# Stored activations moved in 2 KB rows two blocks at a time, and the gate loads of the weighted sum put on ScalarE's DMA queue

## The chip, the core and the metric

One core of one Trainium2 chip. The time is device microseconds of one execution, lower is better. TensorE (PE), VectorE (DVE), ScalarE (ACT), GpSimd (POOL) and SyncE (SP) run their own instruction streams and meet at semaphores; SP, ACT and POOL issue DMAs, each into a queue of its own (q1, q10 and q0 in the profile), and the core's 16 DMA engines serve all three queues.

## The reference, cut to what matters

The program is one inference step of a two-layer network on 384 tokens (128 context, 256 latent) of width 1024. Each layer ends in an expert stage:

```python
q = (x @ w_q).reshape(T, PEER_HEADS, 2, PEER_HALF)          # 8 heads, two halves
s1, i1 = lax.top_k(s[:, :, 0], PEER_TOPK)                   # 16 of 128 keys, each half
...
idx = ...                                                   # 128 of 16384 experts per token
g = jax.nn.softmax(top_s, axis=-1)
uc = jnp.take(u_tab, ic, axis=0)
a = jnp.einsum('cd,ckd->ck', xc, uc)
wgt = gc * jax.nn.gelu(a, approximate=False)
vc = jnp.take(v_tab, ic, axis=0)
return jnp.einsum('ck,ckd->cd', wgt, vc)
```

Both expert tables, u and v, have 16384 rows of 1024 floats (64 MB each, per layer).

## The kernel before

The kernel computes the expert stage in two ways at once.

For the 128 context tokens (the sparse side) POOL gathers, for each of 128 slots, the u row and the v row of every token in one indirect DMA: 128 rows of 8 KB, 1 MB, into one of four buffers that the profile names hf, work, uv_stat and hots (`gather`). DVE takes the dot product with the token (`step`, line 1383), ACT bends it (`weight`, lines 923 and 925), and DVE adds the weighted v row (`add_row`, line 1375), which frees the buffer for a gather four slots later.

For the 256 latent tokens (the dense side) all 16384 experts are evaluated, 128 blocks of 128 experts. A layer's expert stage has these parts:

- **u blocks.** SP loads a block of u (128 rows of 4 KB, 512 KB) into one of four `raw` slots; ACT and POOL split it into a high and a low half (`high`, line 677, and `low`, line 585); PE multiplies; ACT applies GELU (`gelu`, line 908) and stores the block's 128x256 activations in a DRAM tensor `a_dram` (line 910). The slot of `ga` that the GELU writes is one of four, so a GELU waits for the store of four blocks earlier.
- **the table part**, blocks 32 to 95: beside each block PE builds one-hot products of the gates of four tokens, ACT copies them to a staging tile and every eight blocks stores a chunk of the gates to `g_dram` (lines 954 and 955). A gather goes with every second block.
- **the tail**, blocks 96 to 127: no table work, a gather with every block.
- **the sweep**: for each of 128 blocks of v, DVE multiplies the block's activations by its gates (`tt` in `sweep`, line 1423, 128x256, called w below), and PE adds w times v into PSUM (line 1729, four matmuls of 128x512 floats, eight records in the profile). SP loads the v blocks (line 452) four ahead. The activations come back from `a_dram` into four slots of `a_in`: ACT reloads a slot as soon as the w that reads it is done (line 970, 128 rows of 1 KB). The gates come back from `g_dram` for four blocks at a time into two halves of `g_in` (line 542, 1024 pieces of 512 B, 512 KB). SP issues that load after the v load which follows a half's fourth block on PE. A w waits for its slot of `a_in`, for its half of `g_in`, and for the PE block four earlier. A gather goes with every second block.

In the sweep of layer 0 fourteen of the sixteen rounds of eight blocks also load four blocks of `mod_w` of 512 KB (SP, line 554), which DVE reduces (line 1034, twice per block). So a round moves 8 v blocks, 4 gathers, 8 activation blocks, 2 gate halves and 4 mod blocks in layer 0, and the same without the mod blocks in layer 1.

Every queue works in the order in which its engine issues. ACT's program in the sweep is `beside`: in each group of two blocks it waits for w, issues a reload, runs `weight` for the gather of that group, and so on.

Of the kernel before, what the change touches and what calls it, by code (L numbers as in the profile page):

```python
# [33 lines left out]
F32 = mybir.dt.float32  # L34
# [142 lines left out]
def build(nc, io):  # L177
    ctx = ExitStack()
    with ctx:
# [3 lines left out]
        def sem(name):  # L183
            return ctx.enter_context(nc.semaphore(name))
# [64 lines left out]
        mod_w = hots[:, :].rearrange("p (s d) -> p s d", s=MSLOTS)  # L249
        c_all = keys[:, :, :].rearrange("p a k -> p (a k)").rearrange("p (g d) -> p g d", g=2)  # L250
        unread = ga[:, :, :].rearrange("p a t -> p (a t)")[:, 0:D].bitcast(BF16).rearrange("p (g d) -> p g d", g=2)

# [122 lines left out]
        s_taken = sem("s_taken")  # L375
        a_stored = [sem(f"a_stored{j}") for j in range(4)]
        top_ready = sem("top_ready")
# [7 lines left out]
        g_stored = [sem(f"g_stored{j}") for j in range(2)]  # L385
        a_loaded = [sem(f"a_loaded{j}") for j in range(4)]
        g_loaded = [sem(f"g_loaded{j}") for j in range(2)]
# [26 lines left out]

        a_dram = nc.dram_tensor("a_dram", (N_KEYS, P, ND), F32).ap()
        g_dram = nc.dram_tensor("g_dram", (NCHUNK, P, N_KEYS * CHUNK), F32).ap()
# [23 lines left out]
        def _(sp):  # L440
# [63 lines left out]
            for layer in range(DEPTH):  # L504
# [10 lines left out]
                sp.wait_ge(cols_done, layer + 1)  # L515
                for j in range(4):
                    sp.wait_ge(a_stored[j], 16 * (layer * (N_KEYS // 4) + 1))
                    sp.dma_start(a_in[:, j, :], one(a_dram, j)).then_inc(a_loaded[j], 16)
                for s in range(2):
# [3 lines left out]
                for s in range(2):  # L523
                    sp.wait_ge(g_stored[s], 16 * (layer + 1) * (NCHUNK // 2))
                for j in range(4):
                    sp.wait_ge(a_stored[j], 16 * (layer + 1) * (N_KEYS // 4))
# [6 lines left out]
                def beside(i, j, more):  # L533

                    sp.wait_ge(block_done, i * 8 + (v0 + j + 1))
                    if more or j < 8 - RING:
                        load(name, i * 8 + (j + RING), v0 + j)
                    elif after:
                        load(after, j - (8 - RING), v0 + j)
                    if more and j % 4 == 3:  # L540
                        s = j // 4
                        sp.dma_start(g_in[:, s].unsqueeze(1),
                                     g_quads[:, bass.ds(i * 2 + (s + 2), 1)]).then_inc(g_loaded[s], 16)

# [117 lines left out]
        def _(act):  # L662
# [208 lines left out]
            def scores(layer):  # L871
                m0, r0 = M0[f"wq{layer}"], R0[f"wq{layer}"]
                for j in range(4 if layer else 0):
                    act.wait_ge(a_stored[j], 16 * (N_KEYS // 4))
# [28 lines left out]
            def gelu(layer, i, step, m, r, count):  # L903

                j = count % 4
                projected(i, step, m)
                since(act, a_stored[j], i * (4 * step) + 16 * (layer * N_KEYS // 4 + count // 4))
                nc.scalar.activation(ga[:, j, 0:ND], ps[:, PROJ + r % 2, 0:ND], ACT.Gelu).then_inc(proj_taken, 1)  # L908
                act.wait_ge(proj_taken, i * step + (r + 1))
                act.dma_start(one(a_dram, i * step + count), ga[:, j, 0:ND]).then_inc(a_stored[j], 16)  # L910

            def experts(layer):
# [53 lines left out]
                def beside(i, last):  # L966
                    for j in range(8):
                        if j < 4 or not last:
                            act.wait_ge(w_ready, i * 8 + (layer * N_KEYS + j + 1))
                            act.dma_start(a_in[:, j % 4, :], one(a_dram, i * 8 + (j + 4))).then_inc(a_loaded[j % 4], 16)  # L970
                        if j % 2 == 0:
                            weight(i, 4, TABLE_STEPS + TAIL + j // 2)
# [30 lines left out]
        def _(dve):  # L1003
# [409 lines left out]
            def sweep(layer):  # L1413
# [3 lines left out]
                def eight(i, mods):  # L1417
                    for j in range(8):
                        dve.wait_ge(a_loaded[j % 4], i * 32 + (16 * (base // 4 + j // 4 + 1)))
                        if j % 4 == 0:  # L1420
                            dve.wait_ge(g_loaded[j // 4], i * 16 + 16 * (base // 8 + 1))
                        dve.wait_ge(block_done, i * 8 + (v0 + j - WBUFS + 1))
                        tt(wf[:, j % WBUFS, :].rearrange("p (c t) -> p c t", t=CHUNK),  # L1423
                           a_in[:, j % 4, :].rearrange("p (c t) -> p c t", t=CHUNK),
                           g_in[:, j // 4, :, (j % 4) * CHUNK:(j % 4 + 1) * CHUNK], ALU.mult).then_inc(w_ready, 1)
                        if j % 2 == 0:
                            step(layer, i, 4, TABLE_STEPS + TAIL + j // 2)
                        if mods:
                            mod_group(i, MSLOTS, MOD_EARLY - MSLOTS, j // 2, j % 2, mod_late)
# [3 lines left out]
                if layer == 0:  # L1433
                    eight(0, False)
                    settle(nc.vector.memset(a_pad, 0.0))
                    dve.wait_ge(c_ready, 3)
                    for j in range(4):
                        dve.wait_ge(a_stored[j], 16 * (N_KEYS // 4))
# [405 lines left out]
```

## Time and profile before

| | before |
|---|---|
| median of 3 runs | 2580.07 us (2576.76 to 2583.82) |
| the profiled execution | 2576.08 us, span 2573.8 us |
| table part and tail, layer 0 | about 411 to 775 us of the span |
| sweep, layer 0 | about 793 to 1252 us |
| table part and tail, layer 1 | about 1723 to 2090 us |
| sweep, layer 1 | 2109 to 2554 us |
| granted TensorE clock, mean | 0.96 |

The profiled execution is one run of the program, so its own time stands beside its span; 2.3 us lie outside the span. A share of the DMA engines can pass 1, because the records of packets that follow each other on an engine overlap a little.

### The profile page before, as it was taken

To read this page: it belongs to the slowest core of one execution; us is meant where nothing else is said; L and a number is where in the kernel's file an instruction comes from. 1 tells how busy PE (TensorE), PEld (TensorE's weight loads), DVE (VectorE), ACT (ScalarE), POOL (GpSimd) and SP (SyncE) were. 2 spreads that over 40 slices of the span, in tenths; PEclk is the share of its full clock that TensorE was granted. 3 is DMA by queue.
4 is the path that set the end of the run, shared out by engine and by line. 5 is a ranking of instruction groups with operands and counts; after the bars stand their busy time and mean duration, and the time that the engine had idled before them with its cause. 6 is when DMAs were issued, how large, how long until landed. Compare 5 with 4: busy or idle time off the path is not lost.

```text
span 2573.8 us, 40077 instructions
## 1 busy us (share of the span) xinstructions
PE 2300.8 (89%) x11829; PEld 1701.6 (66%) x11829; DVE 1772.7 (69%) x3945; ACT 916.1 (36%) x1702; POOL 1131.7 (44%) x612
## 2 busy tenths in 40 slices
PE   6687999999777989899977889999999769999998
PEld 3676999999773333333467479989998754444443
DVE  7986798888555666666679856888886554444444
ACT  3254445666441111111042453656665420000001
POOL 2623587777782222222145035677777851111110
PEclk8898999999998999999998989999999989999999
DMA  7423378999999999999922023579999999999995
GB/s 295 158 91 116 121 226 306 388 385 382 404 420 396 394 394 394 394 394 394 351 99 90 1 66 115 180 254 368 384 383 384 420 374 370 371 380 381 379 378 206
DMA packets 284090, 771.10 MB, mean 300 GB/s; under 512 B 26080, under 2 KB 160352, under 8 KB 248544
## 3 DMA queue, kind: packets, MB, share of 16 engines
q1 hardware_dynamic: 169664, 401.76, 43.6%
q0 software_dynamic: 36864, 268.45, 25.7%
q10 hardware_dynamic: 77472, 99.78, 10.7%
q8 instruction: 45, 0.74, 0.1%
q14 instruction: 45, 0.37, 0.0%
HBM read 701.08 MB, written 68.81 MB: 299 GB/s over the span
## 4 chain that ended last, share of the span: by engine, by line
PE 54%; DMA 16%; issue 15%; DVE 8%; POOL 4%; SPq 2%; ACT 1%; ACTq 0%; DVEq 0%; POOLq 0%
PE ps L1729 25%; DMA raw<-in_v 7%; PE ps L1495 7%; PE ps L1496 7%; PE ps L1497 7%; PE ps L1711 4%; POOL w_lo L585 4%; DMA work<-in_uv,picked 2%; DMA hf<-in_uv,picked 2%; SPq L554 1%; DMA uv_stat<-in_uv,picked 1%; DMA hots<-in_uv,picked 1%; DVE ga L1034 1%; DVE ps L1375 1%; DMA work<-g_dram 1%
## 5 line engine op out<-in xcount | busy, mean ns | idle before, releaser
L585 POOL TENSOR_TENSOR w_lo<-raw,w_hi 128x1024 fp32r<-128x1024 f32 x330 | 823.1, 2498 | 575.6 <-ACT w_hi L677 573.3
L1729 PE MATMUL ps<-raw,work 128*128 128x512 f32 x2048 | 902.8, 602 | 69.4 <-DMA raw<-in_v 42.5
L1495 PE MATMUL ps<-h_hi,w_hi 128*128 128x256 f32 (+1 forms) x2560 | 781.0, 305 | 92.8 <-POOL w_lo L585 79.6
L1729 PEld LDWEIGHTS ps<-raw,work 128*128 128x128 f32 x2048 | 390.8, 192 | 580.1 <-issue 574.8
L1496 PE MATMUL ps<-h_lo,w_hi 128*128 128x256 f32 (+1 forms) x2560 | 758.3, 296 | 0.0
L1497 PE MATMUL ps<-h_hi,w_lo 128*128 128x256 f32 (+1 forms) x2560 | 758.1, 296 | 0.0
L1495 PEld LDWEIGHTS ps<-h_hi,w_hi 128*128 128x128 f32 x2560 | 495.6, 194 | 112.1 <-POOL w_lo L585 97.4
L1496 PEld LDWEIGHTS ps<-h_lo,w_hi 128*128 128x128 f32 x2560 | 496.2, 194 | 0.0
L1497 PEld LDWEIGHTS ps<-h_hi,w_lo 128*128 128x128 f32 x2560 | 494.9, 193 | 0.0
L677 ACT ACTIVATE w_hi<-raw 128x1024 fp32r<-128x1024 f32 x330 | 348.5, 1056 | 117.5 <-DMA raw<-in_in 36.4
L1423 DVE TENSOR_TENSOR work<-work 128x256 f32<-128x256 f32 x256 | 106.2, 421 | 409.4 <-DMA work<-g_dram 320.9
L923 ACT ACTIVATE wgt<-dots (+1 forms) x256 | 53.2, 208 | 683.9 <-DVE hf L1383 226.6
L603 POOL DMA_INDIRECT hots<-in_uv,picked x64 | 74.5, 1164 | 408.9 <-DVE ps L1375 390.7
L1402 DVE TENSOR_SCALAR hots<-ps,work 128x128 f32<-128x128 f32 x512 | 173.7, 400 | 0.0
L944 ACT ACTIVATE work<-ps 128x512 f32<-128x512 f32 x128 | 145.3, 1135 | 79.5 <-PE ps L1711 64.7
L908 ACT ACTIVATE ga<-ps 128x256 f32<-128x256 f32 x256 | 97.6, 381 | 193.7 <-PE ps L1497 183.5
L603 POOL DMA_INDIRECT work<-in_uv,picked x64 | 71.0, 1110 | 176.5 <-DVE ps L1375 165.8
L1398 DVE TENSOR_TENSOR hots<-ps,work 128x512 f32<-128x512 f32 x128 | 87.9, 687 | 80.4 <-PE ps L1711 80.3
L1034 DVE CUSTOM_DVE_ANT_0 ga<-work,keys 128x1024 bf16<-128x1024 f32 x112 | 136.2, 1216 | 0.0
L1711 PE MATMUL ps<-hots 128*128 128x128 f32 x1024 | 135.4, 275 | 0.0
L603 POOL DMA_INDIRECT uv_stat<-in_uv,picked x64 | 70.9, 1108 | 139.7 <-DVE ps L1375 137.0
L1711 PEld LDWEIGHTS ps<-hots 128*128 128x128 f32 x1024 | 125.6, 192 | 0.4 <-issue 0.2
(195 smaller groups left out, 2315.3 us busy)
## 6 DMA issues: line engine op xcount, KB each, us to landing
raw<-in_u SPq DMA_DIRECT2D x256, 512.0 KB, 6.8
raw<-in_v SPq DMA_DIRECT2D x256, 512.0 KB, 8.9
a_dram<-ga ACTq DMA_DIRECT2D x256, 128.0 KB
work<-g_dram SPq DMA_DIRECT2D x64, 512.0 KB, 11.3
work<-a_dram ACTq DMA_DIRECT2D x248, 128.0 KB, 8.9
g_dram<-work ACTq DMA_DIRECT2D x16, 1920.0 KB, 10.6
work<-in_mod_w SPq DMA_DIRECT2D x56, 512.0 KB, 11.0
hots<-in_mod_w SPq DMA_DIRECT2D x32, 512.0 KB, 3.6
```

The source lines that it names most:

```text
L585: nc.gpsimd.tensor_tensor(w_lo[:, m % RING, :], raw[:, m % RING, :], w_hi[:, m % RING, :].bitcast(F32), ALU.subtract).then_inc(lo_ready, 1)
L603: nc.gpsimd.indirect_dma_start(out=uv_rows[q % UVBUFS], out_offset=None, in_=io[f"uv{layer}"], in_offset=bass.IndirectOffsetOnAxis(ap=pick ...
L677: nc.scalar.activation(w_hi[:, m % RING, :], raw[:, m % RING, :], ACT.Copy).then_inc(hi_ready, 1)
L944: nc.scalar.activation(stage[:, s, :, tok:tok + TOK].rearrange("p k t -> p t k"), ps[:, ACC, :].rearrange("p (t k) -> p t k", k=N_KEYS), A ...
L1034: nc.vector.tensor_tensor_reduce(unread[:, g, :], ring[:, k, :], c_all[:, g, :], 1.0, 0.0, ALU.mult, ALU.add, accum_out=sums[:, k, g:g + 1 ...
L1402: last = ts(oh1[:, b, q, :], iota_p, col_key[:, 0, tok], col_g[:, tok], ALU.is_equal, ALU.mult)
L1423: tt(wf[:, j % WBUFS, :].rearrange("p (c t) -> p c t", t=CHUNK), a_in[:, j % 4, :].rearrange("p (c t) -> p c t", t=CHUNK), g_in[:, j // 4, ...
L1495: mm(out, w_hi[:, s, cols], h_hi[:, k, first:], start=n == 0, stop=False)
L1496: mm(out, w_hi[:, s, cols], h_lo[:, k, first:], start=False, stop=False)
L1497: last = mm(out, w_lo[:, s, cols], h_hi[:, k, first:], start=False, stop=n == KC - 1)
L1711: last = mm(ps[:, ACC, q * P:(q + 1) * P], oh2[:, b, q, :], oh1[:, b, q, :], start=True, stop=True)
L1729: last = mm(ps[:, Y_DENSE[NT - ND_TILES + t] + half, :], wf[:, b, t * P:(t + 1) * P], raw[:, s, half * 512:(half + 1) * 512], start=first, ...
```

## The change

Two things are changed. First, activations travel in pairs. `a_dram` has one row of 2 KB for two blocks where it had two of 1 KB. The GELU of an even block stores nothing; that of the odd block stores both. Reloads too are for two blocks, issued after the w of the odd one. There are two store semaphores and two load semaphores where there were four each. Second, the gate loads of the sweep (but for the first two of a layer) move from SP's program into ACT's `beside`: they are issued behind the reload that follows w of a half's fourth block, where SP issued them after PE had finished that block.

```diff
+        a_out = ga[:, :, :].rearrange("p a t -> p (a t)")[:, 0:4 * ND].rearrange("p (a t) -> p a t", a=4)
...
-        a_dram = nc.dram_tensor("a_dram", (N_KEYS, P, ND), F32).ap()
+        a_dram = nc.dram_tensor("a_dram", (N_KEYS // 2, P, 2 * ND), F32).ap()
...
-                for j in range(4):
+                for j in range(2):
                     sp.wait_ge(a_stored[j], 16 * (layer * (N_KEYS // 4) + 1))
-                    sp.dma_start(a_in[:, j, :], one(a_dram, j)).then_inc(a_loaded[j], 16)
+                    sp.dma_start(a_in[:, 2 * j:2 * j + 2, :].rearrange("p a t -> p (a t)"),
+                                 one(a_dram, j)).then_inc(a_loaded[j], 16)
...
-                    if more and j % 4 == 3:
-                        s = j // 4
-                        sp.dma_start(g_in[:, s].unsqueeze(1),
-                                     g_quads[:, bass.ds(i * 2 + (s + 2), 1)]).then_inc(g_loaded[s], 16)
...
-                since(act, a_stored[j], i * (4 * step) + 16 * (layer * N_KEYS // 4 + count // 4))
-                nc.scalar.activation(ga[:, j, 0:ND], ps[:, PROJ + r % 2, 0:ND], ACT.Gelu).then_inc(proj_taken, 1)
-                act.wait_ge(proj_taken, i * step + (r + 1))
-                act.dma_start(one(a_dram, i * step + count), ga[:, j, 0:ND]).then_inc(a_stored[j], 16)
+                pair = count // 2 % 2
+                since(act, a_stored[pair], i * (4 * step) + 16 * (layer * N_KEYS // 4 + count // 4))
+                nc.scalar.activation(a_out[:, j, :], ps[:, PROJ + r % 2, 0:ND], ACT.Gelu).then_inc(proj_taken, 1)
+                if count % 2:
+                    act.wait_ge(proj_taken, i * step + (r + 1))
+                    act.dma_start(one(a_dram, i * (step // 2) + count // 2),
+                                  a_out[:, j - 1:j + 1, :].rearrange("p a t -> p (a t)")).then_inc(a_stored[pair], 16)
...
-                        if j < 4 or not last:
+                        if j % 2 and (j < 4 or not last):
                             act.wait_ge(w_ready, i * 8 + (layer * N_KEYS + j + 1))
-                            act.dma_start(a_in[:, j % 4, :], one(a_dram, i * 8 + (j + 4))).then_inc(a_loaded[j % 4], 16)
+                            act.dma_start(a_in[:, j % 4 - 1:j % 4 + 1, :].rearrange("p a t -> p (a t)"),
+                                          one(a_dram, i * 4 + (j // 2 + 2))).then_inc(a_loaded[j // 2 % 2], 16)
+                        if j % 4 == 3 and not last:
+                            s = j // 4
+                            act.dma_start(g_in[:, s].unsqueeze(1),
+                                          g_quads[:, bass.ds(i * 2 + (s + 2), 1)]).then_inc(g_loaded[s], 16)
...
-                        dve.wait_ge(a_loaded[j % 4], i * 32 + (16 * (base // 4 + j // 4 + 1)))
+                        if j % 2 == 0:
+                            dve.wait_ge(a_loaded[j // 2 % 2], i * 32 + (16 * (base // 4 + j // 4 + 1)))
```

ACT's program in the sweep, before, from a round's start (line 970 is the activation reload, 923 and 925 are `weight`):

```order
L970 ISA [waits w_ready]
L970 DMA work<-a_dram 128x256
L922 ISA
L923 ISA [waits dot_done]
L923 ACT_TABLE_LOAD
L923 ACTIVATE wgt<-dots 128x1
L925 REGISTER_ALU [waits bent]
L925 ACTIVATE wgt<-wgt,gate_s 128x1
L969 REGISTER_ALU
L970 ISA [waits w_ready]
L970 DMA work<-a_dram 128x256
```

The same program with the change, from the wait for a half's fourth w (line 971 is the reload of a pair, 975 the gate load):

```order
L971 ISA [waits w_ready]
L971 DMA work<-a_dram 128x512
L975 ISA
L975 DMA work<-g_dram 128x8x128
L923 REGISTER_ALU
L924 ISA [waits dot_done]
L924 ACTIVATE wgt<-dots 128x1
L926 REGISTER_ALU [waits bent]
L926 ACTIVATE wgt<-wgt,gate_s 128x1
L970 REGISTER_ALU
L971 ISA [waits w_ready]
L971 DMA work<-a_dram 128x512
```

ACT waits for w once in two blocks and no longer ahead of a round's first `weight`; the gate load stands right behind a reload, and the next pair's reload is behind it in the queue.

SP's program in the sweep of layer 0, before, from the v load that follows a half's third block (line 452 is a v load, 542 the gate load, 554 a mod load):

```order
L452 ISA [waits block_done]
L452 DMA raw<-in_v 128x1024
L535 REGISTER_ALU
L452 ISA [waits block_done]
L452 DMA raw<-in_v 128x1024
L542 ISA
L542 DMA work<-g_dram 128x8x128
L553 REGISTER_ALU
L554 ISA [waits mod_summed]
L554 DMA work<-in_mod_w 128x1024
```

With the change SP's loop has v loads (line 453) and mod loads (line 552) alone:

```order
L453 ISA [waits block_done]
L453 DMA raw<-in_v 128x1024
L537 REGISTER_ALU
L453 ISA [waits block_done]
L453 DMA raw<-in_v 128x1024
L551 REGISTER_ALU
L552 ISA [waits mod_summed]
L552 DMA work<-in_mod_w 128x1024
```

Nothing of SP's queue but the gate load has moved.

ACT's program in the tail, before (line 908 is the GELU, 910 the store, 677 the high half of a later block):

```order
L908 ACTIVATE ga<-ps 128x256 [waits a_stored1,block_done]
L910 DMA a_dram<-ga 128x256 [waits proj_taken]
L923 ACTIVATE wgt<-dots 128x1 [waits dot_done]
L925 ACTIVATE wgt<-wgt,gate_s 128x1 [waits bent]
L677 ACTIVATE w_hi<-raw 128x1024 [waits block_done,raw_ready2]
L908 ACTIVATE ga<-ps 128x256 [waits a_stored2,block_done]
L910 DMA a_dram<-ga 128x256 [waits proj_taken]
```

And with the change (907 is the GELU, 675 the high half):

```order
L907 ACTIVATE ga<-ps 128x256 [waits a_stored0,block_done]
L924 ACTIVATE wgt<-dots 128x1 [waits dot_done]
L926 ACTIVATE wgt<-wgt,gate_s 128x1 [waits bent]
L675 ACTIVATE w_hi<-raw 128x1024 [waits block_done,raw_ready1]
L907 ACTIVATE ga<-ps 128x256 [waits a_stored0,block_done]
L910 DMA a_dram<-ga 128x512 [waits proj_taken]
```

The GELU of an even block now waits for a store that was issued three blocks earlier, where every GELU waited for one issued four blocks earlier.

## Rows read from the trace of the kernel before

**Rows 1.** Windows: busy us per engine, granted clock, DMA share, GB/s

```profile
420.00:640.00 220.00, 220.00 (x1870) 219.92 (x1869) 180.29 (x381) 150.35 (x234) 167.57 (x89) 1.00 0.98 376
660.00:780.00 120.00, 91.14 (x693) 85.67 (x694) 68.69 (x85) 51.06 (x113) 94.52 (x57) 0.99 1.02 419
838.00:1220.00 382.00, 343.26 (x767) 146.24 (x765) 257.82 (x445) 39.27 (x108) 80.13 (x48) 0.98 1.04 394
...
2230.00:2550.00 320.00, 319.10 (x741) 139.60 (x740) 143.50 (x230) 22.88 (x92) 42.49 (x43) 1.00 0.99 368
```

**Rows 2.** The chain that ended last, 930 to 1000 us

```profile
932.46 4.68 SPq L554
937.39 11.49 DMA raw<-in_v
...
949.01 14.01 PE ps L1729 x32
...
963.72 0.38 SPq L542
964.36 5.09 SPq L554
969.71 11.14 DMA raw<-in_v
```

**Rows 3.** PE in time order, 949 to 982 us: start, length, idle before

```profile
949.01 13.99 PE L1729 MATMUL ps<-raw,work 128*128 128x512 f32 x32 [1.77 <-DMA raw<-in_v]
965.17 14.00 PE L1729 MATMUL ps<-raw,work 128*128 128x512 f32 x32 [2.16 <-DMA raw<-in_v]
```

**Rows 4.** DMA queues, 950 to 982 us: packets, MB, share of 16 engines

```profile
q1 hardware_dynamic: 3815, 7.37, 62.2%
q0 software_dynamic: 576, 4.19, 32.4%
q10 hardware_dynamic: 1152, 1.05, 9.5%
```

**Rows 5.** DMA queues, 700 to 750 us, in the tail of layer 0

```profile
q0 software_dynamic: 1753, 12.76, 60.6%
q1 hardware_dynamic: 1796, 6.55, 32.2%
q10 hardware_dynamic: 1739, 1.59, 9.1%
```

**Rows 6.** The chain that ended last, 2075 to 2112 us

```profile
2092.67 0.40 SPq L518
2093.12 0.45 SPq L518
2093.61 0.44 SPq L518
2094.10 0.44 SPq L518
2094.54 0.05 issue
2094.64 13.35 DMA work<-g_dram
```

**Rows 7.** Waits, 665 to 785 us, and the same for 1985 to 2100 us

```profile
ACT ga L908 <- DMA a_dram<-ga: 4.1, 3, 1.7
...
ACT ga L908 <- DMA a_dram<-ga: 5.5, 4, 1.7
```

**Rows 8.** Waits, 838 to 1220 us: total us, times, longest

```profile
DVE work L1423 <- DMA work<-g_dram: 94.3, 13, 7.7
...
PE ps L1729 <- DMA raw<-in_v: 36.8, 19, 2.4
```

**Rows 9.** DMA queues, 974 to 976 us, while gate pieces cross a gather

```profile
q0 software_dynamic: 75, 0.61, 75.1%
q1 hardware_dynamic: 77, 0.11, 15.0%
q10 hardware_dynamic: 77, 0.08, 11.1%
```

**Rows 10.** Gate loads (line 542), 2200 to 2500 us

```profile
DMA to landing us min/median/max: 5.2/8.4/12.1
```

**Rows 11.** DVE in time order, 2303 to 2306 us: a w and one gather's two steps

```profile
2303.27 0.42 DVE L1423 TENSOR_TENSOR work<-work 128x256 f32<-128x256 f32 x1 [11.09 <-DMA work<-g_dram]
2303.61 1.21 DVE L1383 SCALAR_TENSOR_TENSOR hf<-hf,ps 128x1024 f32<-128x1024 f32 x1
2304.75 0.08 DVE L1383 DVE_READ_ACCUMULATOR hf<-hf,ps  x1
2304.75 1.28 DVE L1375 SCALAR_TENSOR_TENSOR ps<-hots,wgt,ps 128x1024 f32<-128x1024 f32 x1
```

More of the change, by code:

```diff
@@ L375, in build @@
         s_taken = sem("s_taken")
-        a_stored = [sem(f"a_stored{j}") for j in range(4)]
+        a_stored = [sem(f"a_stored{j}") for j in range(2)]
         top_ready = sem("top_ready")
@@ L385, in build @@
         g_stored = [sem(f"g_stored{j}") for j in range(2)]
-        a_loaded = [sem(f"a_loaded{j}") for j in range(4)]
+        a_loaded = [sem(f"a_loaded{j}") for j in range(2)]
         g_loaded = [sem(f"g_loaded{j}") for j in range(2)]
@@ L524, in _ @@
                     sp.wait_ge(g_stored[s], 16 * (layer + 1) * (NCHUNK // 2))
-                for j in range(4):
+                for j in range(2):
                     sp.wait_ge(a_stored[j], 16 * (layer + 1) * (N_KEYS // 4))
@@ L872, in scores @@
                 m0, r0 = M0[f"wq{layer}"], R0[f"wq{layer}"]
-                for j in range(4 if layer else 0):
+                for j in range(2 if layer else 0):
                     act.wait_ge(a_stored[j], 16 * (N_KEYS // 4))
@@ L1436, in sweep @@
                     dve.wait_ge(c_ready, 3)
-                    for j in range(4):
+                    for j in range(2):
                         dve.wait_ge(a_stored[j], 16 * (N_KEYS // 4))
```

## The prediction

> **What bounds the kernel now.** I first read the windows by stage [rows 1], because the two edits touch only the expert stages. The reader is to see three kinds of stage there. In the table part (420 to 640 us) PE is busy for the whole window; the DMA engines are nearly full too, but PE sets the pace. In the tail (660 to 780) PE is busy 91 of 120 us and the DMA share is 1.02 at 419 GB/s. In the sweep of layer 0 PE is busy 343 of 382 us with a share of 1.04 at 394 GB/s; in that of layer 1 PE is busy 319.1 of 320 us, and the share is 0.99.
>
> So the sweep of layer 1 holds 0.9 us of idle PE in 320: nothing can be won there but at its start. The one stage with idle PE and moved instructions is the sweep of layer 0. The chain of the end [rows 2] goes there through a v load that SP issued late: SP issued the gate load at 963.72, then stood 5.09 us in the issue of a mod load, and only at 969.71 could the v load begin for which PE waited until 980.85. PE in time order [rows 3] shows 14.0 us of work for four blocks, then about 2 us idle: 16 per half round (965.17 - 949.01 is 16.2), 32 per round. Read alone, this says that the gate load in SP's queue costs 4 us a round.
>
> The DMA queues of the same round [rows 4] say otherwise. The shares sum to 62.2 + 32.4 + 9.5 = 104.1%: all 16 engines work through the whole round, the 2 us in which PE waits included. That is what I take as the limit: 12.6 MB in 32 us. An order of issues that lets the v loads come earlier makes a gather or a gate load come later, and all of them must come within the round, because DVE and the four buffers of each kind let nothing run more than some four blocks ahead.
>
> **The change part by part.** The sum is made against the profiled execution's 2576.08 us (span 2573.8); the median shown is 2580.07, 4 us above it, and I carry the difference over to the median.
>
> *Rows of 2 KB.* No load in the trace has rows of 2 KB, so I interpolate. From the steady tail [rows 5], in which each queue has nearly one size of row: q10 (1 KB) used 9.1% of 16 x 50 = 800 us, 72.8 us for 1590 KB, 45.8 ns per KB; q1 (4 KB) 257.6 us for 6550 KB, 39.3 ns; q0 (8 KB) 484.8 us for 12760 KB, 38.0 ns. A cost of 8.9 ns per row and 37.1 ns per KB fits the first two and gives 38.2 for the third. For 2 KB rows it gives 41.4, that is 4.4 ns less per KB. The ends: no saving at all, or a row as cheap as the 8 KB ones (7.8 ns per KB). In a round of layer 0's sweep the activations are 1049 KB, so 4.6 us of engine time, over 16 engines 0.29 us; fourteen such rounds give **4.0 us**. In the tail, also DMA-bound, a block stores 131 KB: 0.036 us, for 32 blocks in two layers **2.3 us**. In the table part and layer 1's sweep the saving lies beside a busy PE: nothing; it only widens the DMA's slack, by which the next paragraphs are covered.
>
> The Trainium skill (DMA: Bandwidth & Descriptors, Specifications) puts the smallest transfer that runs at line rate at 512 B. By it rows of 1 KB are already at full rate, and the first two terms are nothing; the rows above show 1 KB rows 17% dearer per KB than 4 KB rows, so I don't follow it, but it is a rival below in its own right.
>
> *Fewer issues.* At the start of a sweep SP issues four activation loads, 0.44 us each, ahead of the gate load for which the chain waits in layer 1 [rows 6]. Two of them go: **0.9 us** in layer 1. In layer 0 I count nothing (bound: another 0.9). The issues that ACT loses (four a round) and gains (two a round) are of this kind, some 0.4 us each [rows 2, 6], on an engine that is idle most of the sweep (39 of 382 us busy [rows 1]).
>
> *Stores in pairs.* A GELU's buffer is now asked for three blocks after its store instead of four. In the tail four blocks are just enough at the start, behind the last store of gates: ACT waited for a store 3 times, 4.1 us together, in layer 0 and 4 times, 5.5 us, in layer 1 [rows 7], and nowhere later. A block of the tail takes 4.1 us (12.76 MB of gathers, 1.05 MB each, in 50 us [rows 5]), so at those places the wait can grow by up to 4.1 us. The DMA engines have gathers and u blocks to work on meanwhile, so most of it is covered; I charge **1 us** in all. In the table part PE has a second product buffer, so a GELU can be late by nearly a block's work before PE waits.
>
> *Gate loads on ACT's queue.* The bytes are the same, so in layer 0 the price is nothing as long as the engines stay full. What the move does is to the waits. DVE waits for gates 94.3 us in twelve rounds [rows 8], because SP asks for them only when PE is through the half; ACT can ask when the w is made, up to three blocks sooner. That wait should go or turn into a shorter one for either tensor. But SP's stall behind the gate load goes, ACT gets the stall in its place (behind it: `weight`, for which DVE's next gathered row waits), and the loads compete differently. While gate pieces cross a gather [rows 9] each queue gets the same number of packets, 75 to 77 in 2 us, whatever their size: a 512 B piece costs a turn, in which an 8 KB row passes too. On q10 a gate load (64 pieces per engine) now has two other queues to share with. I take 0, covered by the lead of w.
>
> The sum: 4.0 + 2.3 + 0.9 - 1 = 6.2 us less: 2569.9 for an execution like the profiled one, **2574** for the median. With the ends of the row price (nothing; 7.1 + 4.1 us) the forecast's own range is 2568 to 2580.
>
> **The rivals.**
>
> *SP unblocked pays in full (faster).* If the DMA share of 1.04 hides slack and PE's waits come from the order alone, the waits for v [rows 8], 36.8 us in twelve rounds, go: 43 us for fourteen, 2537; half of it gives 2558. For it: the chain passes through SP's stall. Against it: rows 4 show no free engine time, and the tail's 419 GB/s is reached with longer rows. The Trainium skill says in the same page (Issuing engines are not separate DMA queues) that spreading DMAs over issuing engines saves only issue time. By that this rival is at most the stall itself, where it is not bandwidth.
>
> *The gates starve on q10 (slower).* In layer 1 a half's load is issued after its fourth w and wanted by the w five blocks on; a round is 8 blocks, 28 us at PE's pace (3.5 us each [rows 3]). Between the landing and the next issue for that half lie four w and two gather steps, 4 x 0.42 + 2 x 2.57 = 6.8 us of DVE [rows 11]. So it decides at a landing time of 21 us; each us above costs a us per round, 15 per layer. Before, it was 8.4 us in the median and 12.1 at most [rows 10]. 64 turns at 2 us / (76 / 16) = 0.42 us are 27 us, if both other queues never run dry. Against that: in layer 1 they do, the share being 0.99 of a possible 1.04. At 23 us it would cost 30 us, 2604. By the Trainium skill (same page, Queues, rings and completion order) an engine drains a packet of 9 to 17 descriptors before it turns to another queue; then this rival would be impossible. Rows 9 show single records in turn, so I keep it.
>
> *The store distance (slower).* If a store in the tail's steady part takes over three blocks (12.3 us) but under four, which rows 7 allow, every second GELU is late, and with it the high halves, POOL's low halves and the gathers behind them in POOL's program. At 1 us per pair it is 16 pairs x 2 = 32 us, less the gain: 2606. Against it: q10 passes as many packets as the others in the tail [rows 5], and half of them go, so its backlog should drain.
>
> *The size of a row gives nothing (no change).* Then 2579.
>
> **How the numbers follow.** A measurement of this kernel can tell some 0.3%, 7.7 us, from no change. The forecast gets 0.58; its centre is 1.6 us short of that bound, so I split it 0.20 faster, 0.37 same, 0.01 slower. SP unblocked gets 0.16 (0.15 faster), starved gates 0.10 (0.09 slower), the store distance 0.07 (0.04 slower), no gain from rows 0.09 (0.08 same). Faster 0.36, same 0.50, slower 0.14. The range 2558 to 2590 holds the forecast, half of the first rival and the small ends of the slower ones; it leaves out about 0.18.
>
> **What would show it.** Right: in layer 0's sweep the round shrinks from 32.0 us by some 0.3, the shares still sum to 1.04, and PE still idles near 4 us a round, though SP no longer stands behind a gate load. DVE's wait for gates falls from 94 us in that window by over half. In the tail q10 has half the packets, at about 41 ns per KB. PE stays over 99% busy in layer 1's sweep. Wrong: a round of 29 to 30 us (SP unblocked); PE under 98% in layer 1's sweep with DVE waiting for gates over 20 us after their issue (starved); waits of ACT for stores all through the tail with a block over 4.1 us (store distance).

## The result and the profile after

The changed kernel takes 2622.37 us in the median of 4 runs (2611.35 to 2622.97), the kernel before 2581.95 in the median of its 4. The ratio is 1.0149, with a 95% interval of 1.0123 to 1.0176: slower by 40 us between the medians, where 2574 was forecast with a range of 2558 to 2590. The time is outside the range and on the other side of the kernel before.

The windows by stage of the kernel after, the same stretches as [rows 1]:

```profile
420.00:640.00 220.00, 220.00 (x1871) 220.00 (x1870) 180.62 (x383) 151.35 (x236) 167.29 (x89) 1.00 0.98 377
660.00:780.00 120.00, 92.00 (x692) 86.33 (x690) 69.30 (x87) 51.30 (x112) 93.87 (x57) 0.97 1.02 420
838.00:1220.00 382.00, 321.62 (x695) 138.05 (x694) 229.99 (x397) 35.51 (x97) 71.74 (x43) 0.93 0.95 355
2230.00:2550.00 320.00, 320.00 (x747) 142.10 (x746) 148.14 (x234) 23.38 (x94) 44.93 (x47) 1.00 1.02 382
```

In three of the four rows PE is as busy as before. The third, the sweep of layer 0, is not: the DMA share fell from 1.04 to 0.95 and PE finished 695 matmul records in 382 us instead of 767. A round of eight blocks is 64 records, so the rate gives 35.2 us per round after (382 x 64 / 695) and 31.9 before. From the first matmul of that sweep to the last, PE's rows show 543.5 us where they showed 499.9 (+43.6), some 3.1 us in each of the fourteen rounds. The stretch between the sweeps took 810.3 instead of 815.1 us (-4.8), the sweep of layer 1 442.1 instead of 444.7 (-2.6); with 0.7 us less ahead of the first sweep this is the 35.4 us between the two profiled spans, 2609.2 and 2573.8. (The table of before gives the sweep of layer 0 up to about 1252 us; its last matmul in fact ended at about 1294.)

The mean granted clock in that window fell too, from 0.98 to 0.93 of 2.4 GHz. In the kernels below it is 0.97 to 1.00 where the share is 1.04, 0.95 to 0.97 where it is 1.02 or 1.03, and 0.91 in the slowest. The chain that ended last between 1040 and 1115 us holds no piece of PE at all, so I count no loss of its own for the clock; no run separates the two.

The page's chain names the new cause. Before, DMA of `work<-a_dram` was not in its list; after it is second:

```profile
PE ps L1736 17%; DMA work<-a_dram 12%; PE ps L1502 7%; PE ps L1503 7%; PE ps L1504 6%; PE ps L1718 4%; POOL w_lo L583 3%; DVE ga L1040 3%; DMA work<-in_uv,picked 2%; DVE ps L1381 2%; DMA hots<-in_uv,picked 1%; DMA hf<-in_uv,picked 1%; DMA uv_stat<-in_uv,picked 1%; DVE ps L1328 1%; DVE work L1330 1%
```

The waits of the kernel after, 838 to 1220 us (total us, times, longest), beside [rows 8]:

```profile
DVE work L1430 <- DMA work<-a_dram: 147.4, 19, 12.8
...
PE ps L1736 <- DVE work L1430: 54.6, 10, 8.9
...
PE ps L1736 <- DMA raw<-in_v: 5.7, 7, 1.4
```

DVE (w is line 1430 now) no longer waits for gates; it waits for *activations*, 147 us, where it waited 94 for gates. PE's waits for v fell from 36.8 to 5.7 us, but ten waits for w of up to 8.9 us took their place. The DMA issues of the same window (KB each, median us from issue to landing) say what is late:

```profile
work<-g_dram ACTq DMA_DIRECT2D x22, 512.0 KB, 19.3
...
work<-a_dram ACTq DMA_DIRECT2D x43, 256.0 KB, 10.9
```

And the chain that ended last, 1040 to 1115 us, shows where that sits in a round:

```profile
1050.41 21.13 DMA work<-a_dram
...
1075.93 1.22 DVE ga L1040
...
1078.63 1.20 DVE ps L1381
1079.84 1.13 DVE ga L1040
...
1083.93 1.20 DVE ps L1381
1085.13 1.13 DVE ga L1040
1086.27 0.35 DVE work L1430
1086.77 19.21 DMA work<-a_dram
```

A reload of a pair takes 21.13 us to land. Then DVE works 15 us through w's, gather steps (line 1381) and mod reductions (line 1040) until it has made the w behind which ACT may issue the reload of the same place in the next round, which takes 19.21 us again. 1086.77 - 1050.41 = 36.4 us: a closed loop of one reload and 15 us of DVE per round, longer than the 32 us that the bytes need (the next one takes 35.1 us). In DVE's time order the 15 us hold six w's, three gathers' two steps and five mod reductions, without a gap. ACT's program says why that reload is late, in time order:

```profile
1045.67 0.42 ACTq L975 DMA_DIRECT2D work<-g_dram  x1
...
1050.41 0.35 ACTq L971 DMA_DIRECT2D work<-a_dram  x1
```

It was issued 4.7 us behind a gate load, in the same queue. DVE in time order stood 12.16 us for it:

```profile
1071.77 0.42 DVE L1430 TENSOR_TENSOR work<-work 128x256 f32<-128x256 f32 x1 [12.16 <-DMA work<-a_dram]
```

and PE 5.73 us behind DVE:

```profile
1072.25 4.64 PE L1736 MATMUL ps<-raw,work 128*128 128x512 f32 x5 [5.73 <-DVE work L1430]
```

### The profile page after: what moved, and what is told of

It reads as the page before. It is cut to its first block, busy times and chain, and to the rows that moved or that the text cites. A ratio compares the mean times of both kernels' runs of the same rounds, so it can differ in the third digit from the quotient of the medians.

```text
span 2609.2 us, 39322 instructions
## 1 busy us (share of the span) xinstructions
PE 2309.4 (89%) x11829; PEld 1712.3 (66%) x11829; DVE 1783.1 (68%) x3945; ACT 912.6 (35%) x1702; POOL 1125.7 (43%) x612
## 4 chain that ended last, share of the span: by engine, by line
PE 43%; DMA 20%; DVE 16%; issue 15%; POOL 3%; ACT 1%; DVEq 1%; ACTq 0%; SPq 0%; POOLq 0%
PE ps L1736 17%; DMA work<-a_dram 12%; PE ps L1502 7%; PE ps L1503 7%; PE ps L1504 6%; PE ps L1718 4%; POOL w_lo L583 3%; DVE ga L1040 3%; DMA work<-in_uv,picked 2%; DVE ps L1381 2%; DMA hots<-in_uv,picked 1%; DMA hf<-in_uv,picked 1%; DMA uv_stat<-in_uv,picked 1%; DVE ps L1328 1%; DVE work L1330 1%
## 5 line engine op out<-in xcount | busy, mean ns | idle before, releaser
L1736 PE MATMUL ps<-raw,work 128*128 128x512 f32 x2048 | 912.5, 608 | 100.0 <-DVE work L1430 94.0
L1736 PEld LDWEIGHTS ps<-raw,work 128*128 128x128 f32 x2048 | 398.4, 196 | 612.8 <-issue 523.1
L601 POOL DMA_INDIRECT hf<-in_uv,picked x64 | 70.9, 1107 | 150.1 <-DVE ps L1381 147.0
## 6 DMA issues: line engine op xcount, KB each, us to landing
g_dram<-work ACTq DMA_DIRECT2D x16, 1920.0 KB, 11.1
```

The lines of the kernel that those rows point to most:

```text
L601: nc.gpsimd.indirect_dma_start(out=uv_rows[q % UVBUFS], out_offset=None, in_=io[f"uv{layer}"], in_offset=bass.IndirectOffsetOnAxis(ap=pick ...
L1736: last = mm(ps[:, Y_DENSE[NT - ND_TILES + t] + half, :], wf[:, b, t * P:(t + 1) * P], raw[:, s, half * 512:(half + 1) * 512], start=first, ...
```

## The experiments

The theory after the result: a gate load is 1024 pieces of 512 B, 64 on each DMA engine, and each costs its queue a turn. On ACT's queue the pair's reload stands behind these turns, and in layer 0 DVE's share of the loop is long, because the mod reductions are in it. The rivals: that the pairs do it (rows of 2 KB, the store distance, two slots asked for at a time); that the reload behind the gates is at fault and the order in the queue would mend it; that the load on DVE or on the DMA engines alone has grown. Of each kernel below the text names the window 838 to 1220 us of layer 0's sweep, unless it says otherwise. Ratios are against the kernel before on the same chip, whose median was 2581.2, 2581.9 and 2581.9 us in the three groups of runs.

**pairs_only**: the change without the move of the gate loads.

```diff
+                    if more and j % 4 == 3:
+                        s = j // 4
+                        sp.dma_start(g_in[:, s].unsqueeze(1),
+                                     g_quads[:, bass.ds(i * 2 + (s + 2), 1)]).then_inc(g_loaded[s], 16)
...
-                        if j % 4 == 3 and not last:
-                            s = j // 4
-                            act.dma_start(g_in[:, s].unsqueeze(1),
-                                          g_quads[:, bass.ds(i * 2 + (s + 2), 1)]).then_inc(g_loaded[s], 16)
```

> The pairs of blocks and the 2 KB rows, with the gate loads back in SP's program. Theory A (the reload of a pair waits in ScalarE's queue behind the gate load, and DVE's next round waits for it): layer 0's round is DMA-bound again, 31.5 to 32 us instead of 35; the time is 2 to 10 us under the kernel before, ratio 0.996 to 1.000. Theory B (the pairs are at fault: a reload is asked for one w later and lands as a whole): most of the 40 us stay, ratio 1.010 or more. Theory C (both edits share the loss): ratio near 1.007.

2570.46 us (2567.32 to 2574.19), ratio 0.9958 (0.9944 to 0.9971). The pairs cost nothing and save some 11 us. Its windows:

```profile
838.00:1220.00 382.00, 347.58 (x773) 148.09 (x772) 258.05 (x445) 39.26 (x108) 79.76 (x48) 0.97 1.04 398
```

and its waits:

```profile
DVE work L1430 <- DMA work<-g_dram: 86.6, 14, 8.3
```

The share is back at 1.04, and DVE waits for gates as in [rows 8], with a gate load landing in 11.3 us on SP's queue.

**gates_only**: the kernel before with nothing but the move of the gate loads; rows of 1 KB, one block at a time.

```diff
-                    if more and j % 4 == 3:
-                        s = j // 4
-                        sp.dma_start(g_in[:, s].unsqueeze(1),
-                                     g_quads[:, bass.ds(i * 2 + (s + 2), 1)]).then_inc(g_loaded[s], 16)
...
+                        if j % 4 == 3 and not last:
+                            s = j // 4
+                            act.dma_start(g_in[:, s].unsqueeze(1),
+                                          g_quads[:, bass.ds(i * 2 + (s + 2), 1)]).then_inc(g_loaded[s], 16)
```

> Single blocks and 1 KB rows as before, with the gate loads on ScalarE's queue behind the reload of a half's fourth block. Theory A: the reload of the next block stands behind the gate load, so the loss is there, ratio 1.010 to 1.018, DVE waiting some 10 us a round in layer 0 for activations or gates. Theory B: the loss is gone, ratio 0.998 to 1.002. Theory C: near 1.007.

2622.09 us (2615.56 to 2623.76), ratio 1.0153 (1.0136 to 1.017): all of the loss, without a single 2 KB row. Its windows:

```profile
838.00:1220.00 382.00, 323.11 (x685) 137.27 (x684) 229.34 (x397) 35.50 (x97) 71.78 (x43) 0.92 0.96 357
```

and its waits:

```profile
DVE work L1423 <- DMA work<-a_dram: 150.6, 11, 15.1
```

The two halves of the change are not additive. Alone the move costs 1.53% and the pairs give 0.42%, together it is 1.49%. On top of the pairs the move thus costs some 1.9%, about 50 us. A likely reason, only argued: where the loop through DVE sets the round, bytes that cross faster are worth little.

**gate_rows_4k**: the kernel after, but ACT's gate load brings its 512 KB as 128 rows of 4 KB from one place of `g_dram` (the gates are then not those of the block, so the weighted sum differs).

```diff
-                            act.dma_start(g_in[:, s].unsqueeze(1),
-                                          g_quads[:, bass.ds(i * 2 + (s + 2), 1)]).then_inc(g_loaded[s], 16)
+                            act.dma_start(g_in[:, s].rearrange("p c t -> p (c t)"),
+                                          one(g_dram, 0)[:, 0:NCHUNK * QUAD * CHUNK]).then_inc(g_loaded[s], 16)
```

> The changed kernel, but every gate load issued by ScalarE reads 128 rows of 4 KB (the same 512 KB, from one place of the stored gates) instead of 1024 pieces of 512 B; the gates that it multiplies are thus not the right ones. Theory A, in which a piece costs a turn between the queues: 8 turns instead of 64, the gate load lands in under 12 us instead of 19, layer 0's round falls to the DMA bound, which is itself 1 us lower for 1792 fewer records a round: ratio 0.987 to 0.995. If the turn plays no part and the load is slow for its bytes or its place: landing near 19 us, ratio near 1.015.

2558.91 us (2558.01 to 2560.56), ratio 0.9914 (0.9899 to 0.9929). Same bytes, same queue, same place in it, an eighth of the pieces. Its DMA issues:

```profile
work<-g_dram ACTq DMA_DIRECT2D x25, 512.0 KB, 11.1
```

and its waits:

```profile
DVE work L1430 <- DMA work<-a_dram: 13.3, 7, 2.7
```

The landing falls from 19.3 to 11.1 us, DVE's wait from 147 to 13 us. So it is the cut into small pieces, not the queue or the order as such. The edit also reads one place of DRAM over and over; that alone did not make records short, as a 4 KB record of this load held its engine 168 ns and one of SP's loads from fresh places 165.

By the Trainium skill (DMA: Bandwidth & Descriptors, Specifications) pieces of 512 B are already at line rate. The trace's packet records decide against it: in this window of the kernel after, a 512 B piece held its engine 28.6 ns, so eight of them 229 ns against the 168 of one 4 KB record. For two gate loads a round that is 58.6 against 43.0 us of engine time, 1.0 us over 16 engines. It accounts for a quarter of the 3.8 us by which the round is shorter here (31.4 by the 779 records); the rest is the shorter landing.

**mod_sums_short**: the kernel after, with DVE reducing 64 of the 1024 columns of each later mod block (the sums of `mod` are then partial); the loads stay whole.

```diff
-                nc.vector.tensor_tensor_reduce(unread[:, g, :], ring[:, k, :], c_all[:, g, :], 1.0, 0.0,
+                n = 64 if ring is mod_late else D
+                nc.vector.tensor_tensor_reduce(unread[:, g, 0:n], ring[:, k, 0:n], c_all[:, g, 0:n], 1.0, 0.0,
```

> The changed kernel, but DVE reduces only 64 of 1024 columns of each mod block in layer 0's sweep (all loads are kept; the later modulation values are thus wrong). Theory A, a loop of queue time and DVE's ordered work (w, gather steps, mod reductions of 1.2 us each): with some seven reductions less in the loop the round falls from 35 us to the DMA bound near 32, ratio 0.998 to 1.003. If the loss is in the queues alone, whatever DVE does: the round stays near 35, ratio 1.012 or more.

2578.17 us (2575.18 to 2583.43), ratio 0.9993 (0.9984 to 1.0002). The loads are as slow as after, and the loop is shorter. Its windows:

```profile
838.00:1220.00 382.00, 339.55 (x751) 145.74 (x751) 164.83 (x446) 39.27 (x108) 48.32 (x48) 0.96 1.02 388
```

and its chain, 1040 to 1115 us:

```profile
1044.58 21.05 DMA work<-a_dram
...
1077.06 22.05 DMA work<-a_dram
```

21 to 22 us of landing are still on the chain, but the same reload comes every 32.5 us instead of every 36.4. So DVE's reductions are part of the loop. DVE waits for activations even longer than after, 207.4 us in this window, and the kernel is as fast as before: the sum of its waits is no measure of the loss. The edit has one side effect that it does not separate: POOL's gather instructions take 1.01 us on average instead of 1.67. 751 records give a round of 32.6 us, not the 31.6 of pairs_only: the queue's part is still just long enough to be felt.

**mod_loads_small**: the kernel after, with SP loading 64 of 1024 columns of each later mod block (so `mod` is made from stale columns); DVE reduces all columns. The load is still of 128 pieces, each of 256 B instead of 4 KB.

```diff
-                                sp.dma_start(mod_late[:, j // 2, :], one(io["mod_w"], i * MSLOTS + (MOD_EARLY + j // 2))
+                                sp.dma_start(mod_late[:, j // 2, 0:64],
+                                             one(io["mod_w"], i * MSLOTS + (MOD_EARLY + j // 2))[:, 0:64]
```

> The changed kernel, but in layer 0's sweep SP loads 64 of 1024 columns of each further mod block; DVE still reduces all 1024 columns (of old data, so the later modulation values are wrong). Theory A, a loop of queue time plus some 15 us of DVE's ordered work: DVE's part stays, the queue part falls towards the 13 us that a gate load takes in layer 1, so the round is near 28 us and bound by PE; ratio 0.970 to 0.980 (14 rounds less 7 us of after is 98 us from 2622). If DVE's work alone were the bound the round would stay at 35.

2514.38 us (2511.16 to 2518.29), ratio 0.9738 (0.9724 to 0.9752). Its windows:

```profile
838.00:1220.00 382.00, 382.00 (x891) 169.14 (x890) 300.74 (x514) 45.04 (x127) 90.99 (x55) 1.00 1.04 388
```

and its DMA issues:

```profile
work<-g_dram ACTq DMA_DIRECT2D x27, 512.0 KB, 11.4
```

PE is busy for the whole window. The queue order, the full DVE loop and the number of pieces are as after, but the four mod loads of a round bring 0.13 MB instead of 2.1, and a gate load lands in 11.4 us. So neither a long DVE loop nor the gates on ACT's queue lose time alone; the two need long records on the other queues. The edit also lowers the time that a round's bytes need, and does not separate this from the sooner turns.

**gates_behind**: the kernel after, with each gate load issued behind a reload that the next w's need, not ahead of it: after the sixth and eighth w of a round.

```diff
-                        if j % 4 == 3 and not last:
-                            s = j // 4
+                        if j in (5, 7) and not last:
+                            s = (j - 5) // 2
```

> The changed kernel, but the gate load of the first half is issued behind the reload of the pair that the same w will need (after the sixth w instead of the fourth). Theory A1 (w needs both, and whatever stands last in ScalarE's queue ends its wait): the reload lands in under 12 us, but the gates, asked for 5 us later, land as late as the reload did: DVE's wait is now for the gates, round 35 us or more, ratio 1.012 to 1.022. Theory A2 (only the reload's place behind the gate load hurts): round near 32, ratio 1.000 to 1.005.

2643.61 us (2634.4 to 2645.45), ratio 1.0231 (1.0213 to 1.0249), slower yet. Its waits change their name and hardly their length:

```profile
DVE work L1430 <- DMA work<-g_dram: 134.0, 10, 16.2
...
DVE work L1430 <- DMA work<-a_dram: 18.6, 9, 3.4
```

Now the gate load itself, 19.6 us from issue to landing, ends the wait. This reordering within ACT's queue does not mend the loss. It also asks for the gates two blocks later than the kernel after, three w's ahead of their use instead of five, so the run does not say what the order alone is worth.

**gates_sp_early**: pairs_only, with SP issuing the gate load two blocks earlier, behind a wait for w instead of for PE.

```diff
-                    if more and j % 4 == 3:
+                    if more and j % 4 == 1:
                         s = j // 4
+                        sp.wait_ge(w_ready, i * 8 + (layer * N_KEYS + j + 3))
```

> Pairs as in pairs_only, gate loads in SP's queue, but asked for as early as the changed kernel does: after the w of a half's fourth block instead of after its PE block. Theory A (the queue that they share, not the time at which they are asked for): as pairs_only, ratio 0.994 to 0.999, DVE's wait for gates in layer 0 falls from 87 us to under 40. If asking early crowds out the v loads: PE waits for v, layer 0's round 33 us or more, ratio 1.003 or more.

2580.33 us (2573.36 to 2586.08), ratio 0.9995 (0.9984 to 1.0006). DVE's wait for gates falls from 86.6 to 21.0 us and the rounds get no shorter. DVE waits for PE instead, 92.7 us where pairs_only has 6.4, and PE's wait for v goes from 26.6 to 34.2 us:

```profile
DVE work L1431 <- PE ps L1737: 92.7, 34, 7.2
...
PE ps L1737 <- DMA raw<-in_v: 34.2, 19, 3.4
DVE work L1431 <- DMA work<-g_dram: 21.0, 11, 2.6
```

So the 94 us that DVE waited for gates before [rows 8] were not a cost. Why it is some 10 us behind pairs_only is not settled. Its steady round is as long between w's of the rounds 3 to 15 (31.8 us in both), though its window has 759 records instead of 773 and a granted clock of 0.95 instead of 0.97; and from the 113th w to the last it takes 57.8 us, where pairs_only takes 48.4.

**before_again** and **pairs_only_again**: the two kernels unchanged, to see what such differences are worth.

> The kernel before once more, under a label of its own: ratio 1.000 within 0.002. Its profile shows how far the stages of one and the same kernel differ between two executions; pairs_only's profiled execution was 5 us faster than that of before, its median 10.7 us. If the profiled execution shown for before was a fast one of its kind, this one has 3 to 6 us more, spread over stages that no edit touches.

> pairs_only once more, beside the other two on the same chip: ratio 0.994 to 0.9975, and 102 us for the first 32 blocks of layer 1.

2579.93 us, ratio 0.9997 (0.9988 to 1.0007); and 2572.26, ratio 0.9962 (0.9947 to 0.9976), in another group of runs than pairs_only with 0.9958. The gain of the pairs repeats. Of the two profiles of the kernel before, one has a round of 31.9 us by its records (767 in 382 us), the other 31.8 (770); pairs_only and its repetition have 31.6 (773 both).

**reload_pairs**: pairs_only, with the stores single again (1 KB into one half of a 2 KB row, four semaphores); only the reloads are of 2 KB.

```diff
-                if count % 2:
-                    act.wait_ge(proj_taken, i * step + (r + 1))
-                    act.dma_start(one(a_dram, i * (step // 2) + count // 2),
-                                  a_out[:, j - 1:j + 1, :].rearrange("p a t -> p (a t)")).then_inc(a_stored[pair], 16)
+                act.wait_ge(proj_taken, i * step + (r + 1))
+                half = slice(count % 2 * ND, (count % 2 + 1) * ND)
+                act.dma_start(one(a_dram, i * (step // 2) + count // 2)[:, half], a_out[:, j, :]).then_inc(a_stored[j], 16)
```

> Gate loads in SP's queue; only the reloads are of pairs (2 KB rows); every block is stored by itself again, as 1 KB halves of the 2 KB rows, with four store semaphores. It splits pairs_only's gain. Theory D (the reloads give 0.2 us a round in layer 0's sweep, and the stores give 3 us at the start of layer 1's expert stage, where ACT's own issues lie in the chain): the first 32 blocks of layer 1 take 105 us as before, not 102; the round is 31.75 us; ratio 0.997 to 0.9995, less gain than pairs_only by 3 to 6 us. If the stores play no part: ratio 0.995 to 0.9965, as pairs_only.

2573.47 us (2570.03 to 2577.5), ratio 0.997 (0.9959 to 0.9981), against 0.9962 for pairs_only_again beside it. The two intervals overlap: between the medians the paired stores give 1.2 us, and anything from nothing to some 7 us would fit. The profiles show a difference in the first 32 u blocks of layer 1, in which ACT is on the chain before. Windows over exactly these blocks, of the kernel before:

```profile
1621.00:1726.00 105.00, 96.92 (x767) 93.88 (x766) 92.09 (x348) 64.01 (x80) 80.51 (x36) 0.98 0.72 232
```

and of pairs_only:

```profile
1618.50:1720.50 102.00, 94.85 (x766) 93.43 (x765) 97.07 (x346) 62.25 (x80) 80.24 (x36) 0.98 0.74 240
```

The same 80 instructions of ACT and the same matmuls take 3 us less. In the chain of before, 1640 to 1700 us, ACT's store issue (line 910) holds 6.9%; with half the issues DVE's top-k leads there. From the 1st GELU of layer 1 to the 33rd it is 104.9 us in both profiles of the kernel before and in reload_pairs, 102.0 in both of pairs_only, and 102.0 to 103.0 in the other kernels with paired stores. So the profiles give these 2 to 3 us to the paired stores; the medians neither confirm nor exclude it.

**gates_by_layer**: pairs_only, with SP issuing the gate loads in layer 0 and ACT in layer 1.

```diff
-                    if more and j % 4 == 3:
+                    if more and j % 4 == 3 and not layer:
...
+                        if j % 4 == 3 and not last and layer:
+                            s = j // 4
+                            act.dma_start(g_in[:, s].unsqueeze(1),
+                                          g_quads[:, bass.ds(i * 2 + (s + 2), 1)]).then_inc(g_loaded[s], 16)
```

> Pairs, with the gate loads in SP's queue in layer 0 and in ScalarE's in layer 1, where DVE has no mod reductions in its loop. Theory A (the loss needs DVE's long loop): no loss in layer 1; the sweep of layer 1 took 442.1 us with ScalarE's queue and 445.7 with SP's, so 1 to 4 us under pairs_only, ratio 0.993 to 0.9965. If the early gate loads cost in layer 1 as well: above pairs_only by 3 us or more.

2568.3 us (2567.41 to 2570.72), ratio 0.9952 (0.9939 to 0.9965), the lowest of the kernels that leave nothing out, though its interval overlaps that of pairs_only_again (0.9962). On ACT's queue the gates cost layer 1 nothing, though DVE waits 141.2 us for activations there between 2250 and 2550 us. In the kernel after they land there, 2250 to 2550 us, so:

```profile
DMA to landing us min/median/max: 9.9/13.0/17.3
```

13.0 us where [rows 10] had 8.4, at no cost to a PE that is busy for 320.00 of 320 us in the window of the kernel after.

## Why the prediction was wrong

**The step that failed** is *Gate loads on ACT's queue*: "in layer 0 the price is nothing as long as the engines stay full", and "I take 0, covered by the lead of w". The engines did not stay full: 0.95 instead of 1.04. The step was worth +41 us alone (gates_only, 1.0153) and about +50 on top of the pairs (1.0149 against 0.9958 for pairs_only), and not 0. I read full engines [rows 4] as a property of the stage; they were one of the state in which enough transfers were in flight. DVE, the four activation slots and ACT's issues form a loop, and a loop that is longer than the byte time empties the queues.

**The rival was the right mechanism in the wrong layer.** "The gates starve on q10" had the loop, the condition ("decides at a landing time of 21 us", "each us above costs a us per round") and a landing of 23 to 27 us, of which 21.1 came true for what stands behind the gates. But I worked DVE's part out from [rows 11], in layer 1, as 6.8 us, and added the rival's price there. In layer 0 it was 15 us on the chain. Five mod reductions of 1.22 us each make most of the difference; the rest is that the loop closes over the reload behind the gates, and so holds six w's and three gathers where I had counted four and two. With 32 - 15 = 17 us to land in, 21.1 and 19.2 lose 2 to 4 us a round, and the records say 3.3. Layer 1, with some 10 us by the same count without reductions (6 x 0.42 + 3 x 2.57, [rows 11]) and a landing of 13.0 of its 28 us, has room to spare, and its sweep lost nothing. I had also overlooked that the w's wait is not only for the gates: the reload of the next pair stands behind them, and in gates_behind, where the w's wait for the gates instead, nothing is gained.

**Single records in turn.** The Trainium skill (DMA: Bandwidth & Descriptors, Queues, rings and completion order) lets an engine drain a packet of 9 to 17 descriptors before it turns to another queue. The trace does not agree. If the packet records around 975 us of the kernel before are put in line, each start to the end that it follows, an engine's sizes read 512 B, 1 KB, 8 KB, 512 B, 1 KB, 8 KB: one record of each queue in turn, as the equal counts of [rows 9] suggested. The prediction's step from the page's rule to "then this rival would be impossible" was not sound either. 64 pieces would need 4 to 7 turns, but each turn would wait for 9 to 17 records of 161 and 311 ns (the prices of [rows 5]) of the other queues, some 30 us in all. The estimate of 27 us for 64 single turns was too long: 19.3 were measured, 0.30 us a turn.

**Rows of 2 KB.** Priced at 41.4 ns per KB. The DMA queues of the kernel after in the tail, 700 to 750 us:

```profile
q10 hardware_dynamic: 864, 1.57, 8.2%
```

8.2% of 800 us for 1570 KB are 41.8 ns: the interpolation held. What it is worth did not. The tail shows no gain (126.9 us in layer 0 and 127.2 in layer 1 from its first GELU to the last, 127.2 and 126.9 before), where 2.3 us were forecast for the two layers together; but before_again has 131.2 and 128.4, so two profiles cannot settle such a term. The round of pairs_only is 31.6 to 31.9 us where 0.29 less than before was forecast: by the records 0.2 to 0.3, by the times of w 0.0 to 0.2. Yet the pairs gave 10 to 11 us in the median, more than my 6.2. In the profiles about 3 are in layer 1's first blocks, with ACT's issues, a term that I did not have, and the sweep of layer 0 is 1.7 shorter in its matmuls (498.2 against 499.9; the repetitions have 497.9 and 502.0). The profiled spans differ by only 5.1 us (2568.7 against 2573.8) and 6.6 (the repetitions, 2570.8 against 2577.4). Where the rest of the medians' difference lies is open. (Two small slips of the prediction's sums: at the two ends of the row price the range is 2569 to 2580, not 2568, and with no gain from rows 2580, not 2579.)

**Fewer issues of SP.** 0.9 us forecast; the stretch between the sweeps is 4.8 us shorter after, of which 2.0 lie in layer 1's first 32 blocks (102.9 us instead of 104.9). It fits, and is no more than that.

**Stores in pairs.** 1 us charged, and none is to be seen. Waits for stores in the kernel after, 665 to 785 us, beside the 4.1 us of [rows 7]:

```profile
ACT ga L907 <- DMA a_dram<-ga: 2.5, 1, 2.5
```

The rival of the store distance falls with it, as the lead of three blocks never ran out in the tail.

**SP unblocked.** SP's stall behind the gate load did go (its mod issues took 0.53 us at most in the window, one was 5.09 in [rows 2]), and in gates_sp_early DVE's wait for gates went too. Neither shortened a round of 31.8 us. This bears out the reading of [rows 4], that bytes set the pace before.

## What to carry to other kernels

Before moving a transfer to another queue, write down the loop that it joins: landing time behind everything that stands ahead of it there, plus what the engines do until the same transfer is issued again, and do so in *each* stage with that stage's own instructions; a DMA share near 1 is no cover, since a loop longer than the byte time empties the engines. Count a strided load by its pieces and not by its bytes: keep small pieces out of the queue on which something with a short lead depends, or make them larger. A long wait in the profile, as DVE's 94 us for gates here, can be what the bytes cost anyway, and removing it is worth nothing until something else is the bound.

## What the runs showed of the hardware

A 512 KB load of 512 B pieces took 19.3 us to land among two busy queues, the same load in 4 KB rows 11.1 us, and again 11.4 us with 512 B pieces once the mod blocks' records on the other queue were 256 B instead of 4 KB. The engine itself was held 28.6 ns by a 512 B piece, 64 of them 1.8 us; so most of the 19.3 us is waiting, and the wait grows with what the other queues pass meanwhile. Moving the load from SP's queue to ACT's changed its landing from 11.3 (pairs_only) to 19.3 us at the same bytes and from the same DRAM. A likely reason, only argued, is that on SP's queue the pieces stand in line with the v and mod loads, which otherwise compete with them from another queue.
